# The first projection by quarters, and the constants behind the second and third weight blocks

## The chip, the cores and the metric

One core of a Trainium2 chip runs the whole program in one launch. The metric is the device time of one execution in microseconds (us), lower is better. The kernel before took 724.19 us as the median of three runs (722.73 to 724.41).

## The reference

A two-layer transformer over 256 tokens of width 1024, in float32. Layer 0 is a differential attention with eight heads, followed by a mixture of 32 experts (two chosen per token); layer 1 is a latent attention (MLA) and a second mixture. Only the start of layer 0 is touched here:

```python
q, k, v = jnp.split(x @ w_qkv, 3, axis=-1)          # x: 256 x 1024, w_qkv: 1024 x 3072
...
logits = einsum('bqhcd,bkhcd->bhcqk', q, k)          # two score maps for each of 8 heads
logits = where(chunk_causal, logits - slopes * dist, -inf)
p = softmax(logits)
a = p[:, :, 0] - lam_full * p[:, :, 1]               # lam_full from exp of two dot products
o = rmsnorm(a @ v, subln_g) * (1 - lambda_init)      # then @ w_o, residual, layer norm, experts
```

## The kernel before, in words

All five engines run programs written out by hand; each waits on semaphores. There is no scheduler: the order in the source is the order of execution on each engine, and an instruction that waits holds up all that stand behind it on its engine.

**Split products.** A float32 product is made of three products in a rounded format: operand `a` is written as `a_hi + a_lo`, and `products` (L580) issues hi·hi, hi·lo and lo·hi. ScalarE (ACT) casts to make the upper part, VectorE (DVE) subtracts to make the remainder, TensorE (PE) multiplies.

**The weights of the first attention** come as six blocks of 1024 x 512 (2 MB each) on SyncE's DMA queue (SP, L440 to L454). Block 0 comes in three pieces: rows of quarter 0, of quarter 1, of quarters 2 and 3 (`ld_qkv0`), with semaphores of their own; blocks 1 to 5 have `ld_qkv[c]`. The large constants `cst` (404.5 KB) are queued between block 1 and block 2. GpSimd (POOL) loads nine small tensors (`load_small`, L2209): the triangle and the distance matrix, `diff_lambda`, the router's bias, and the scales of the norms as columns. It begins when the first piece of block 0 has landed. These transfers share the 16 DMA engines with the weights.

**The order at the start.** PE runs 14 dummy products (`keep_clock(START_WAIT)`), transposes `x` (L577) into four PSUM banks, waits for all four remainders of `x` (`x_copied`), runs 8 dummy products (`FIRST_WAIT`), and then goes through four quarters of the inner dimension: for each it waits for the remainder of the weights (`w_lo_ready`) and issues 24 products, so 96 for block 0. ACT casts the four parts of `x` (L1190) and then the four quarters of block 0 (L1208). DVE makes the four remainders of `x` (L1687) and then the four of the weights (L1707).

**Behind it.** PE runs `project_heads(1, 0..2)` (24 products each, block 1), `scores(0)`, `project_heads(1, 3)`, `scores(1)`, `project_values(2, ...)` and so on, with the softmax of head h between the products of later blocks. ACT: `upper(1)`, `move(0)`, `upper(2)`, `move(2)`, `upper(3, (0, 1))`, `exps(0)`, ... DVE: `lower(1)`, `move(1)`, `lower(2)`, `constants()`, `lower(3, (0, 1))`, `logits(0)`, `move(3)`, `lambda_ready()`, ... Here `upper` and `lower` are the cast and the subtraction of a quarter of a block (L1216, L1714), `move(g)` copies a finished group out of PSUM, `logits(h)` takes the maxima of head h (L1736), `exps(h)` the exponentials (L1230), `probabilities(h)` (L1750) the difference of the two maps. PE's `scores(0)` waits for `lam_ready`, the last step of `constants()`. `transposes(h)` (L657) waits for `probabilities(h)`; `values(0)` waits for `move(5)` (L1702).

**After the attention,** the loads of the experts' weights are issued by SP when PE has finished given groups (`qkv_ps`, `wo_ps`, `gu_ps`).

Of the kernel before, what the change touches and what calls it, by code (L numbers as in the profile page):

```python
# [30 lines left out]
ALU = mybir.AluOpType  # L31
# [3 lines left out]
P = 128  # L35
SEQ = 256
TT = SEQ // P
D = 1024
KD = D // P
# [29 lines left out]
RAW_BANKS = ((4, 5, 2, 3), (4, 5, 6, 7))  # L69
ROW_BANK = (6, 3)  # L70
REST_BANK = (4, 6)
START_WAIT, FIRST_WAIT, NORM_WAIT, TOP_WAIT, SORT_WAIT = 14, 8, (11, 0), 6, 8


GU = KD * FF
# [11 lines left out]
CONSTS = _at  # L87
# [62 lines left out]
def build(nc, consts, x, diff_w_qkv, diff_lambda, diff_subln_g, diff_w_o, mla_w_kv_a, mla_kv_norm_g, mla_w_kv_b,  # L150
          mla_w_q_a, mla_q_norm_g, mla_w_q_b, mla_w_o, router_w, router_b, moe_w_gate, moe_w_up, moe_w_down,
          ln_g, ln_b, out):
    with ExitStack() as ctx:
# [10 lines left out]
        def sem(name):  # L164
            return ctx.enter_context(nc.semaphore(name))


        ring, ring_r = zip(*(sb_and_rounded(f"ring{s}", [P, SLOT]) for s in range(SLOTS)))
        xs = sb("x_res", [P, TT, D])
        xT, xT_r = sb_and_rounded("x_T", [P, KD, SEQ])  # L170
# [38 lines left out]
        def qkv_chunk(r, c):  # L209
            a = (c % 3) * 4096  # L210
            return r[2 - c // 3][:, a:a + 4096].rearrange("p (k n) -> p k n", k=KD)
# [110 lines left out]


        ld_x, ld_wo, ld_rw = sem("ld_x"), sem("ld_wo"), sem("ld_router")
        MISC = 8
        ld_ident, ld_cst, ld_misc, ld_lam = sem("ld_ident"), sem("ld_cst"), sem("ld_misc"), sem("ld_lam")

        x_hi_ready, w_hi_ready, w_lo_ready, w_pool_ready = (
            sem(n) for n in ("x_hi_ready", "w_hi_ready", "w_lo_ready", "w_pool_ready"))
# [16 lines left out]
        def x_copied(n):  # L346
            return xt[0]["sb"], KD * {0: 1, 1: 2, 3: 3}[n]
# [94 lines left out]
        def _(sp):  # L442
# [6 lines left out]
            for c in range(1, 6):  # L449
                cols = slice(QKV_COLS[c] * 512, (QKV_COLS[c] + 1) * 512)  # L450
                sp.dma_start(qkv_chunk(ring, c), wq[:, :, cols]).then_inc(ld_qkv[c], 16)
                if c == 1:
                    sp.dma_start(cst[:, P:], consts[:, P:CONSTS]).then_inc(ld_cst, 16)

            def load_wo(w, at_):
# [104 lines left out]
        def _(pe):  # L560
# [8 lines left out]
            def transpose_x(n):  # L569

                for t in range(TT):
                    if n:
                        keep_clock(NORM_WAIT[t], (4, 0)[t])
                        pe.wait_ge(*ln[n - 1]("norm", (1, 3)[t]))
                    for k in range(KD):
                        at_ = (k % 2) * SEQ + t * P
                        last = pe.transpose(psum[:, 4 + k // 2, at_:at_ + P], xs[:, t, k::KD], ident)  # L577
                        if t and k % 2:
                            last.then_inc(xt[n]["ps"], 1)
                if n != 2:  # L580
                    pe.wait_ge(*x_copied(n))

            def products(dst, lhsT, rhs, first, last):

                (a_hi, a_lo), (b_hi, b_lo) = lhsT, rhs
                mm(dst, a_hi, b_hi, first, False)
                mm(dst, a_hi, b_lo, False, False)
                return mm(dst, a_lo, b_hi, False, last)

            def diff_attention():  # L590
# [5 lines left out]

                keep_clock(FIRST_WAIT, 0)
                for q in range(4):
                    pe.wait_ge(w_lo_ready, q + 1)
                    for m in range(4):  # L600
                        for k in (2 * q, 2 * q + 1):
                            cols = slice(m * P, (m + 1) * P)
                            last = products(psum[:, m, 0:SEQ], (w_hi[:, 0, k, cols], qkv_chunk(ring_r, 0)[:, k, cols]),
                                            (xT_r[:, k, :], x_lo[:, k, :]), k == 0, k == KD - 1)
                        if q == 3 and m % 2:
                            last.then_inc(qkv_ps, 1)
                def project_heads(c, m):
                    g = 2 * c + m // 2
                    if m % 2 == 0 and g >= 4:
# [544 lines left out]
        def _(act):  # L1154
# [30 lines left out]
                normalise(1, slice(0, D // 2))  # L1185

            def diff_attention():
                for b in range(4):
                    act.wait_ge(*xt[0]("ps", b + 1))
                    act.copy(xT_r[:, 2 * b:2 * b + 2, :], psum[:, 4 + b, :].rearrange("p (k t) -> p k t", k=2))\  # L1190
                       .then_inc(x_hi_ready, 1)

                def move(g):

# [7 lines left out]
                        c = g // 6  # L1202
                        act.copy(v[:, 0, c * 512:(c + 1) * 512], psum[:, 6, :]).then_inc(qkv_act, 1)

                for q in range(4):
                    act.wait_ge(ld_qkv0[min(q, 2)], 16)
                    rows = slice(2 * q, 2 * q + 2)
                    act.copy(w_hi[:, 0, rows, :], qkv_chunk(ring, 0)[:, rows, :]).then_inc(w_hi_ready, 1)  # L1208
                def upper(c, ms):

                    for m in ms:
# [290 lines left out]
            act.copy(ln_sd[:, 0:1], eps[:, :])  # L1502

            diff_attention()
            act.wait_ge(ld_misc, 16 * MISC)
            moe(0)
            sum_layer_norm(1)
            mla_attention()
# [7 lines left out]
        def _(dve):  # L1516
# [155 lines left out]
                dve.memset(eps[:, :], EPS).then_inc(lam_ready, 1)  # L1672
            def constants():
                dve.wait_ge(ld_cst, 16)
                dve.tensor_copy(ones_b[:, :], ones).then_inc(cast_ready, 1)
                dve.wait_ge(ld_misc, 16 * MISC)
                dve.tensor_copy(tri_b[:, :], tri_f).then_inc(cast_ready, 1)
                dve.tensor_copy(dist_b[:, :], dist_f)

                dve.wait_ge(ld_lam, 16)  # L1680
                chain(dve.tensor_tensor(lam_prod, lam_in[:, 0::2, :], lam_in[:, 1::2, :], ALU.mult))
                dve.tensor_reduce(lam_dot, lam_prod, AX.X, ALU.add).then_inc(lam_ready, 1)

            def diff_attention():
                for b in range(4):
                    dve.wait_ge(x_hi_ready, b + 1)
                    dve.tensor_tensor(x_lo[:, 2 * b:2 * b + 2, :], psum[:, 4 + b, :].rearrange("p (k t) -> p k t", k=2),  # L1687
                                      xT_r[:, 2 * b:2 * b + 2, :], ALU.subtract).then_inc(xt[0]["sb"], 2)

                def move(g):  # L1690

                    dve.wait_ge(qkv_ps, g + 1)
                    src, kind = qkv_heads(g), g // 2 % 3
                    if kind == 0:
                        dve.tensor_scalar(qT[:, heads_of(g), :], src, DH ** -0.5, None, ALU.mult).then_inc(qkv_dve, 1)
                    elif kind == 1:
                        dve.tensor_copy(kT[:, heads_of(g), :], src).then_inc(qkv_dve, 1)
                    else:
                        c = g // 6
                        if c:  # L1700
                            dve.wait_ge(cast_ready, 3)
                        dve.tensor_copy(v[:, 1, c * 512:(c + 1) * 512], psum[:, 7, :]).then_inc(qkv_dve, 1)  # L1702

                for q in range(4):
                    dve.wait_ge(w_hi_ready, q + 1)
                    rows = slice(2 * q, 2 * q + 2)
                    dve.tensor_tensor(qkv_chunk(ring_r, 0)[:, rows, :], qkv_chunk(ring, 0)[:, rows, :],  # L1707
                                      w_hi[:, 0, rows, :], ALU.subtract).then_inc(w_lo_ready, 1)
                def lower(c, ms):

                    for m in ms:
# [5 lines left out]
                def lambda_ready():  # L1717

                    dve.wait_ge(lam_exp, 1)
                    chain(dve.tensor_tensor(nlam[:, :], lam_dot[:, 1:2], lam_dot[:, 0:1], ALU.subtract))  # L1720
                    chain(dve.tensor_scalar(nlam[:, :], nlam[:, :], LAMBDA_INIT, None, ALU.subtract))
                    chain(dve.tensor_scalar(subg[:, :], subg[:, :], 1.0 - LAMBDA_INIT, None, ALU.mult))
# [55 lines left out]

                lower(1, range(4))
                move(1)  # L1780
                lower(2, range(4))
                constants()
                lower(3, (0, 1))
                dve.wait_ge(lam_ready, 2)
                logits(0)
# [349 lines left out]
        def _(pool):  # L2135
# [72 lines left out]

            def load_small():  # L2209

                pool.dma_start(tri_f, consts[:, CONSTS:CONSTS + P]).then_inc(ld_misc, 16)
                pool.dma_start(dist_f, consts[:, CONSTS + P:CONSTS + 4 * P]).then_inc(ld_misc, 16)
                pool.dma_start(lam_in, diff_lambda[0].partition_broadcast(P)).then_inc(ld_lam, 16)
                pool.dma_start(rb[:, :], router_b.partition_broadcast(P)).then_inc(ld_misc, 16)
                with nc.allow_non_contiguous_dma(reason="norm scales as columns, once"):
                    pool.dma_start(subg[:, :], diff_subln_g[0].rearrange("(p a) -> p a", a=1)).then_inc(ld_misc, 16)
                    pool.dma_start(qg[:, :], mla_q_norm_g[0].rearrange("(k p) -> p k", p=P)).then_inc(ld_misc, 16)
                    pool.dma_start(kvg[:, :], mla_kv_norm_g.rearrange("(k p) -> p k", p=P)).then_inc(ld_misc, 16)
                    for col, w in ((gcol, ln_g), (bcol, ln_b)):
                        pool.dma_start(col[:, :, :], w.rearrange("l j (p k) -> p (l j) k", k=KD)[:, 0:3, :])\  # L2220
                          .then_inc(ld_misc, 16)

            pool.wait_ge(ld_qkv0[0], 16)
            load_small()

            def squares(h):
# [11 lines left out]
                pool.dma_start(rw, router_w.rearrange("(p k) n -> p k n", k=KD)).then_inc(ld_rw, 16)  # L2238

            pool.wait_ge(ld_ident, 16)  # L2240
            for h in range(4):
                slopes(h)
            squares(0)
            slopes(4)
# [45 lines left out]
```

## Time and profile before

| | |
|---|---|
| median of three runs | 724.19 us |
| the profiled execution: its own time / span | 722.91 us / 721.1 us |
| granted TensorE clock, mean | 0.987 |
| PE busy | 679.4 us, 94% |
| DVE / ACT / POOL busy | 331.2 / 212.4 / 129.6 us |
| DMA | 237.66 MB, mean 330 GB/s |

The profile is one execution. Times are from the start of its span. In a timeline each row is: start, duration, engine, line, operation, tiles, count, and in brackets how long the engine was idle before and what ended that. Rows of like instructions are merged, so that a row's start plus its duration is the end of the last of them; neighbouring instructions of one engine overlap by some tens of ns.

### The profile page before, as it was taken

Reading aid. Unit: us, or ns where it says so; the run is one execution under the profiler, and the core shown is the slowest. Engines: PE = TensorE matmul, PEld = TensorE weight load, DVE = VectorE, ACT = ScalarE, POOL = GpSimd, SP = SyncE. Lnnn points to the kernel's source line nnn. Section 1 sums busy time; section 2 is a strip of 40 time slices with the busy share of each in tenths; the row PEclk is TensorE's granted clock in tenths of the full one; section 3 lists DMA queues with packets and bytes.
Section 4 is the critical chain, followed back from the end, with each engine's and each line's share of the span. In section 5 each row is a group of like instructions: output and inputs, shape, how many; then the busy total and the mean of one; then the engine's idle time right before and its main releaser. Section 6 shows DMA issues by size and latency. Waiting matters only on the chain.

```text
span 721.1 us, 9996 instructions
## 1 busy us (share of the span) xinstructions
PE 679.4 (94%) x3617; PEld 384.5 (53%) x3617; DVE 331.2 (46%) x679; ACT 212.4 (29%) x416; POOL 129.6 (18%) x143
## 2 busy tenths in 40 slices
PE   7999999889999999999989898988999999999993
PEld 5879878463343343435546776846333334333551
DVE  4658755743434233242274755674343423323226
ACT  4558660421111111111155145342111211112112
POOL 4004010152110010100029560015211101010000
PEclk9999999999999999999999999999999999999997
DMA  8990049959999999999995019385999999999991
GB/s 304 381 357 2 1 187 402 372 204 359 425 421 422 422 420 422 422 422 422 423 413 202 0 44 422 126 349 215 360 424 421 421 421 422 422 422 422 420 404 62
DMA packets 40168, 237.66 MB, mean 330 GB/s; under 512 B 3824, under 2 KB 4000, under 8 KB 15040
## 3 DMA queue, kind: packets, MB, share of 16 engines
q1 hardware_dynamic: 39120, 235.37, 80.1%
q10 hardware_dynamic: 576, 1.05, 0.4%
q0 software_dynamic: 432, 0.70, 0.4%
q8 instruction: 25, 0.41, 0.2%
q14 instruction: 15, 0.12, 0.0%
HBM read 236.06 MB, written 1.05 MB: 329 GB/s over the span
## 4 chain that ended last, share of the span: by engine, by line
PE 88%; DVE 7%; issue 2%; ACT 2%; POOL 1%; POOLq 0%; DVEq 0%; ACTq 0%
PE psum L562 85%; PE psum L1022 2%; POOL scratch L2182 1%; DVE ln_stats L1616 1%; DVE work L1953 1%; DVE work L431 1%; PE psum L872 1%; ACT scratch L1471 0%; PE psum L577 0%; PE psum L657 0%; DVE x_T L1581 0%; POOLq L2166 0%; DVE scratch L1906 0%; DVE ring_rounded L1687 0%; DVE small L1909 0%
## 5 line engine op out<-in xcount | busy, mean ns | idle before, releaser
L562 PE MATMUL psum<-ring,work 128*64 128x512 f32 (+2 forms) x1296 | 231.3, 506 | 3.9 <-DVE work L2047 3.9
L562 PEld LDWEIGHTS psum<-ring,work 128*64 128x64 f32 (+1 forms) x1296 | 94.3, 138 | 137.9 <-issue 116.8
L562 PE MATMUL psum<-ring,scratch 128*64 128x512 f32 x512 | 116.9, 598 | 3.7 <-ACT scratch L1471 3.7
L2089 DVE TENSOR_TENSOR scratch<-psum,scratch 128x256 f32<-128x256 f32 x32 | 13.6, 425 | 183.2 <-ACT scratch L1467 183.2
L2167 POOL COPY work<-work 128x512 f32 x60 | 37.4, 626 | 302.5 <-PE psum L562 295.8
L1460 ACT ACTIVATE x_T_rounded<-psum,small 128x512 fp32r<-128x512 f32 x64 | 43.8, 688 | 110.1 <-DVE scratch_rounded L2070 75.7
L562 PEld LDWEIGHTS psum<-ring,scratch 128*64 128x64 f32 x512 | 33.9, 136 | 68.8 <-issue 63.6
L1467 ACT ACTIVATE scratch<-psum 128x256 f32<-128x256 f32 x32 | 12.3, 384 | 195.1 <-PE psum L562 195.1
L562 PE MATMUL psum<-ring_rounded 128*128 128x256 f32 (+1 forms) x214 | 66.1, 309 | 0.0
L562 PE MATMUL psum<-x_T_rounded,scratch_rounded 128*128 128x512 f32 x144 | 63.1, 438 | 1.9 <-ACT x_T_rounded L1460 1.4
L562 PE MATMUL psum<-ring_rounded,x_T_rounded 128*128 128x512 f32 x192 | 60.7, 397 | 0.0
L562 PE MATMUL psum<-x_T_rounded,ring_rounded 128*128 128x256 f32 x256 | 48.0, 286 | 0.0
L562 PEld LDWEIGHTS psum<-x_T_rounded,scratch_rounded 128*128 128x128 f32 x144 | 29.5, 205 | 31.0 <-issue 28.1
L562 PEld LDWEIGHTS psum<-ring_rounded 128*128 128x128 f32 x214 | 41.5, 194 | 2.0
L562 PEld LDWEIGHTS psum<-x_T_rounded,ring_rounded 128*128 128x128 f32 x256 | 40.4, 192 | 0.8 <-DVE ring_rounded L1714 0.3
L562 PEld LDWEIGHTS psum<-ring_rounded,x_T_rounded 128*128 128x128 f32 x192 | 35.3, 189 | 8.0 <-issue 1.3
L2074 DVE SCALAR_TENSOR_TENSOR work_rounded<-psum,small,x_T_rounded 128x512 fp32r<-128x512 f32 x32 | 24.0, 751 | 28.3 <-ACT x_T_rounded L1460 28.3
L2074 DVE SCALAR_TENSOR_TENSOR scratch_rounded<-psum,small,x_T_rounded 128x512 fp32r<-128x512 f32 x32 | 24.0, 750 | 16.2 <-ACT x_T_rounded L1460 15.9
L2061 DVE SCALAR_TENSOR_TENSOR scratch<-x_T,cst 128x256 f32<-128x256 f32 x32 | 15.7, 491 | 27.2 <-PE psum L562 27.2
L1714 DVE TENSOR_TENSOR ring_rounded<-ring,ring_rounded 128x1024 fp32r<-128x1024 f32 x20 | 23.8, 1241 | 8.1 <-ACT ring_rounded L1216 8.1
L562 PE MATMUL psum<-scratch_rounded 128*128 128x512 f32 x64 | 25.3, 396 | 0.0
L562 PE MATMUL psum<-work_rounded,scratch_rounded 128*128 128x512 f32 x64 | 25.3, 396 | 0.0
(265 smaller groups left out, 850.0 us busy)
## 6 DMA issues: line engine op xcount, KB each, us to landing
ring<-in_moe_w_gate SPq DMA_DIRECT2D x64, 1024.0 KB, 15.6
ring<-in_moe_w_up SPq DMA_DIRECT2D x64, 1024.0 KB, 19.6
ring<-in_moe_w_down SPq DMA_DIRECT2D x64, 1024.0 KB, 20.6
ring<-in_diff_w_qkv SPq DMA_DIRECT2D x5, 2048.0 KB, 19.5
ring<-in_diff_w_o SPq DMA_DIRECT2D x1, 4096.0 KB, 15.7
ring<-in_mla_w_o SPq DMA_DIRECT2D x1, 4096.0 KB, 35.3
ring<-in_mla_w_q_b SPq DMA_DIRECT2D x1, 2304.0 KB, 28.9
ring<-in_mla_w_kv_b SPq DMA_DIRECT2D x1, 2048.0 KB, 27.8
```

The source lines that it names most:

```text
L431: link(eng.tensor_tensor(dst[:, :, lo], src[:, :, lo], c, ALU.mult))
L562: return pe.matmul(dst, lhsT, rhs, start=start, stop=stop, skip_group_check=True)
L872: last = pe.transpose(psum[:, 2 + h % 2, b * P:(b + 1) * P], mlg[h % 3][:, b * P:(b + 1) * P], ident)
L1022: last = pe.transpose(psum[:, 7, k * P:(k + 1) * P], h_sb[:, k::FF // P], ident)
L1460: act.activation(y_hi[:, c * 512:(c + 1) * 512], psum[:, 4 + c, :], ACT.Copy, scale=gate_col)\
L1467: act.activation(act_s, psum[:, 6, 0:FF], ACT.Silu).then_inc(m["s_ready"], 1)
L1616: chain(dve.bn_stats(ln_stats[:, t, c, :], psum[:, 2 * t + c, :]))
L1714: dve.tensor_tensor(qkv_chunk(ring_r, c)[:, :, cols], qkv_chunk(ring, c)[:, :, cols], w_hi[:, c % 2, :, cols], ALU.subtract).then_inc(w_lo ...
L2061: dve.scalar_tensor_tensor(out=comb, in0=key_row[:, 0, :], scalar=at_, in1=gate_row[:, 0, :], op0=ALU.is_equal, op1=ALU.mult).then_inc(par ...
L2074: dve.scalar_tensor_tensor(out=y_lo[c], in0=psum[:, 4 + c, :], scalar=gate_col, in1=y_hi[:, c * 512:(c + 1) * 512], op0=ALU.mult, op1=ALU. ...
L2089: dve.tensor_tensor(h_sb, psum[:, 6, FF:2 * FF], act_s, ALU.mult).then_inc(m["h_ready"], 1)
L2167: last = pool.tensor_copy(xg[:, buf, :, j * WIN:(j + 1) * WIN], xsT[:, :, bass.ds(a, WIN)])
```

## The change

Block 0 is worked on by quarters on ACT and DVE (cast of `x`, cast of weights; remainder of `x`, remainder of weights), and PE issues in each quarter first the eight hi·hi products, then the eight with the remainder of `x`, then the eight with the remainder of the weights, each with its own wait. PE no longer waits for all of `x_lo`, and runs 3 dummy products instead of 8. `cst` is queued behind block 2. POOL's transfers wait for block 1 instead of the first piece of block 0; the six for scales and the router's bias are issued later still, behind the first two `slopes`. On DVE `constants()` stands ahead of `lower(2)`, and waits for `cst` and the three small tensors.

```diff
-START_WAIT, FIRST_WAIT, NORM_WAIT, TOP_WAIT, SORT_WAIT = 14, 8, (11, 0), 6, 8
+START_WAIT, FIRST_WAIT, NORM_WAIT, TOP_WAIT, SORT_WAIT = 14, 3, (11, 0), 6, 8
@@ sync
                 sp.dma_start(qkv_chunk(ring, c), wq[:, :, cols]).then_inc(ld_qkv[c], 16)
-                if c == 1:
+                if c == 2:
                     sp.dma_start(cst[:, P:], consts[:, P:CONSTS]).then_inc(ld_cst, 16)
@@ tensor
-                if n != 2:
-                    pe.wait_ge(*x_copied(n))
...
                 for q in range(4):
+                    def first_products(w, src, first, last):
+                        for m in range(4):
+                            for k in (2 * q, 2 * q + 1):
+                                done = mm(psum[:, m, 0:SEQ], w[:, k, m * P:(m + 1) * P], src[:, k, :],
+                                          first and k == 0, last and k == KD - 1)
+                            if last and q == 3 and m % 2:
+                                done.then_inc(qkv_ps, 1)
+                    pe.wait_ge(w_hi_ready, q + 1)
+                    first_products(w_hi[:, 0], xT_r, True, False)
+                    pe.wait_ge(*xt[0]("sb", 2 * (q + 1)))
+                    first_products(w_hi[:, 0], x_lo, False, False)
                     pe.wait_ge(w_lo_ready, q + 1)
-                    for m in range(4):
-                        for k in (2 * q, 2 * q + 1):
-                            cols = slice(m * P, (m + 1) * P)
-                            last = products(psum[:, m, 0:SEQ], (w_hi[:, 0, k, cols], qkv_chunk(ring_r, 0)[:, k, cols]),
-                                            (xT_r[:, k, :], x_lo[:, k, :]), k == 0, k == KD - 1)
-                        if q == 3 and m % 2:
-                            last.then_inc(qkv_ps, 1)
+                    first_products(qkv_chunk(ring_r, 0), xT_r, False, True)
@@ scalar
+                for q in range(4):
+                    rows = slice(2 * q, 2 * q + 2)
+                    act.wait_ge(*xt[0]("ps", q + 1))
+                    act.copy(xT_r[:, rows, :], psum[:, 4 + q, :].rearrange("p (k t) -> p k t", k=2)).then_inc(x_hi_ready, 1)
+                    act.wait_ge(ld_qkv0[min(q, 2)], 16)
+                    act.copy(w_hi[:, 0, rows, :], qkv_chunk(ring, 0)[:, rows, :]).then_inc(w_hi_ready, 1)
@@ vector: remainders of x and of the weights in one loop over q, in the same way; constants() ahead of lower(2)
             def constants():
                 dve.wait_ge(ld_cst, 16)
+                dve.wait_ge(ld_small, 16 * 3)
...
                 def lambda_ready():
                     dve.wait_ge(lam_exp, 1)
+                    dve.wait_ge(ld_scales, 16 * SCALES)
@@ gpsimd
-            pool.wait_ge(ld_qkv0[0], 16)
+            pool.wait_ge(ld_qkv[1], 16)
             load_small()                      # now three transfers: triangle, distances, lambda
             pool.wait_ge(ld_ident, 16)
-            for h in range(4):
+            for h in range(2):
+                slopes(h)
+            load_scales()                     # the other six
+            for h in range(2, 4):
                 slopes(h)
```

## Rows read from the trace of the kernel before

**Rows 1.** Chain that ended last, in order of time: start, us, what (count).

```profile
11.35 22.06 PE psum L562 x176
33.41 1.22 issue
47.34 0.33 PE psum L657 x3
```

**Rows 2.** The same chain by engine, from the page.

```profile
PE 88%; DVE 7%; issue 2%; ACT 2%; POOL 1%; POOLq 0%; DVEq 0%; ACTq 0%
```

**Rows 3.** Timeline of TensorE: dummy products, first products, then values(0) and values(2).

```profile
11.35 1.90 PE L562 MATMUL psum<-zeros_b 128*128 128x512 bf16 x8 [2.60 <-DVE ring_rounded L1687]
...
13.21 0.28 PE L562 MATMUL psum<-ring_rounded 128*128 128x256 f32 x1
...
13.57 0.28 PE L562 MATMUL psum<-ring_rounded 128*128 128x256 f32 x1
...
57.55 0.83 PE L562 MATMUL psum<-work,scratch 128*128 128x128 f32 x6
...
65.30 0.83 PE L562 MATMUL psum<-work,scratch 128*128 128x128 f32 x6
```

**Rows 4.** Timeline of ScalarE, 0 to 65 us.

```profile
8.12 2.06 ACT L1190 CAST x_T_rounded<-psum 128x512 fp32r<-128x512 f32 x4 [5.83 <-PE psum L577]
10.03 4.14 ACT L1208 CAST ring_rounded<-ring 128x1024 fp32r<-128x1024 f32 x4
12.17 2.00 ACT L1208 CAST ring_rounded<-ring 128x1024 fp32r<-128x1024 f32 x2
21.38 3.90 ACT L1216 CAST ring_rounded<-ring 128x1024 fp32r<-128x1024 f32 x4 [7.21 <-DMA ring<-in_diff_w_qkv]
...
27.76 3.90 ACT L1216 CAST ring_rounded<-ring 128x1024 fp32r<-128x1024 f32 x4 [1.99 <-DMA ring<-in_diff_w_qkv]
...
33.18 1.99 ACT L1216 CAST ring_rounded<-ring 128x1024 fp32r<-128x1024 f32 x2 [1.05 <-DMA ring<-in_diff_w_qkv]
...
63.49 0.37 ACT L1241 COPY work<-psum 128x256 f32<-128x256 f32 x1
```

**Rows 5.** Timeline of VectorE, 0 to 60 us.

```profile
8.81 2.48 DVE L1687 TENSOR_TENSOR ring_rounded<-psum,x_T_rounded 128x512 fp32r<-128x512 f32 x4 [7.61 <-ACT x_T_rounded L1190]
...
28.84 4.63 DVE L1714 TENSOR_TENSOR ring_rounded<-ring,ring_rounded 128x1024 fp32r<-128x1024 f32 x4 [1.14 <-ACT ring_rounded L1216]
...
34.45 2.35 DVE L1714 TENSOR_TENSOR ring_rounded<-ring,ring_rounded 128x1024 fp32r<-128x1024 f32 x2
36.71 1.02 DVE L1736 TENSOR_REDUCE small<-psum 128x2 f32<-128x256 f32 x2
...
44.07 0.75 DVE L1750 SCALAR_TENSOR_TENSOR scratch<-scratch,small 128x128 f32<-128x128 f32 x2 [2.47 <-ACT scratch L1237]
...
51.69 1.02 DVE L1736 TENSOR_REDUCE small<-psum 128x2 f32<-128x256 f32 x2 [0.45 <-PE psum L562]
...
55.85 0.69 DVE L1702 COPY work<-psum 128x512 f32<-128x512 f32 x1
```

**Rows 6.** Timeline of GpSimd: first and third of the nine small transfers issued.

```profile
8.38 0.73 POOL L2211 DMA_DIRECT2D work<-in_shape_constants  x1 [7.88 <-DMA ring<-in_diff_w_qkv]
...
9.64 0.56 POOL L2213 DMA_DIRECT2D scratch<-in_diff_lambda  x1
```

**Rows 7.** DMA issues of two small transfers: KB, us from issue to landing.

```profile
scratch<-in_diff_lambda POOLq DMA_DIRECT2D x1, 128.0 KB, 7.3
ln_b_cols<-in_ln_b POOLq DMA_DIRECT2D x1, 12.0 KB, 8.1
```

**Rows 8.** Stretches: busy us of each engine (instructions), granted clock, DMA share, GB/s.

```profile
16.00:18.00 2.00, 2.00 (x19) 2.00 (x18) 0.02 (x1) 0.00 (x0) 0.41 (x1) 1.00 0.85 274
...
24.00:26.00 2.00, 2.00 (x19) 2.00 (x18) 2.00 (x3) 1.77 (x3) 0.00 (x0) 1.00 1.06 389
```

**Rows 9.** Waits of SyncE's queue up to 160 us: in total, times, longest.

```profile
SPq L466 <- PE psum L562: 90.9, 3, 59.0
```

More of the change, by code:

```diff
@@ L324, in build @@
         ld_x, ld_wo, ld_rw = sem("ld_x"), sem("ld_wo"), sem("ld_router")
-        MISC = 8
-        ld_ident, ld_cst, ld_misc, ld_lam = sem("ld_ident"), sem("ld_cst"), sem("ld_misc"), sem("ld_lam")
+        SCALES = 6
+        ld_ident, ld_cst, ld_scales, ld_small = sem("ld_ident"), sem("ld_cst"), sem("ld_scales"), sem("ld_small")
         x_hi_ready, w_hi_ready, w_lo_ready, w_pool_ready = (
@@ L1187, in diff_attention @@
             def diff_attention():
[L1188 to L1191, printed above, removed]
+                for q in range(4):
[4 more added lines that the diff above has]
+                    act.copy(w_hi[:, 0, rows, :], qkv_chunk(ring, 0)[:, rows, :]).then_inc(w_hi_ready, 1)
                 def move(g):
@@ L1203, in move @@
                         act.copy(v[:, 0, c * 512:(c + 1) * 512], psum[:, 6, :]).then_inc(qkv_act, 1)
[L1205 to L1208, printed above, removed]
                 def upper(c, ms):
@@ L1504, in _ @@
             diff_attention()
-            act.wait_ge(ld_misc, 16 * MISC)
+            act.wait_ge(ld_scales, 16 * SCALES)
             moe(0)
@@ L1674, in constants @@
                 dve.wait_ge(ld_cst, 16)
+                dve.wait_ge(ld_small, 16 * 3)
                 dve.tensor_copy(ones_b[:, :], ones).then_inc(cast_ready, 1)
-                dve.wait_ge(ld_misc, 16 * MISC)
                 dve.tensor_copy(tri_b[:, :], tri_f).then_inc(cast_ready, 1)
                 dve.tensor_copy(dist_b[:, :], dist_f)
-                dve.wait_ge(ld_lam, 16)
                 chain(dve.tensor_tensor(lam_prod, lam_in[:, 0::2, :], lam_in[:, 1::2, :], ALU.mult))
@@ L1684, in diff_attention @@
             def diff_attention():
[L1685 to L1688, printed above, removed]
+                for q in range(4):
+                    rows = slice(2 * q, 2 * q + 2)
+                    dve.wait_ge(x_hi_ready, q + 1)
+                    dve.tensor_tensor(x_lo[:, rows, :], psum[:, 4 + q, :].rearrange("p (k t) -> p k t", k=2),
+                                      xT_r[:, rows, :], ALU.subtract).then_inc(xt[0]["sb"], 2)
+                    dve.wait_ge(w_hi_ready, q + 1)
+                    dve.tensor_tensor(qkv_chunk(ring_r, 0)[:, rows, :], qkv_chunk(ring, 0)[:, rows, :],
+                                      w_hi[:, 0, rows, :], ALU.subtract).then_inc(w_lo_ready, 1)
                 def move(g):
@@ L1702, in move @@
                         dve.tensor_copy(v[:, 1, c * 512:(c + 1) * 512], psum[:, 7, :]).then_inc(qkv_dve, 1)
[L1704 to L1708, printed above, removed]
                 def lower(c, ms):
@@ L1780, in diff_attention @@
                 move(1)
+                constants()
                 lower(2, range(4))
-                constants()
                 lower(3, (0, 1))
@@ L2209, in load_small, with load_scales @@
             def load_small():
[L2211 to L2214, printed above, removed]
+                pool.dma_start(tri_f, consts[:, CONSTS:CONSTS + P]).then_inc(ld_small, 16)
+                pool.dma_start(dist_f, consts[:, CONSTS + P:CONSTS + 4 * P]).then_inc(ld_small, 16)
+                pool.dma_start(lam_in, diff_lambda[0].partition_broadcast(P)).then_inc(ld_small, 16)
+            def load_scales():
+                pool.dma_start(rb[:, :], router_b.partition_broadcast(P)).then_inc(ld_scales, 16)
                 with nc.allow_non_contiguous_dma(reason="norm scales as columns, once"):
-                    pool.dma_start(subg[:, :], diff_subln_g[0].rearrange("(p a) -> p a", a=1)).then_inc(ld_misc, 16)
-                    pool.dma_start(qg[:, :], mla_q_norm_g[0].rearrange("(k p) -> p k", p=P)).then_inc(ld_misc, 16)
-                    pool.dma_start(kvg[:, :], mla_kv_norm_g.rearrange("(k p) -> p k", p=P)).then_inc(ld_misc, 16)
+                    pool.dma_start(subg[:, :], diff_subln_g[0].rearrange("(p a) -> p a", a=1)).then_inc(ld_scales, 16)
+                    pool.dma_start(qg[:, :], mla_q_norm_g[0].rearrange("(k p) -> p k", p=P)).then_inc(ld_scales, 16)
+                    pool.dma_start(kvg[:, :], mla_kv_norm_g.rearrange("(k p) -> p k", p=P)).then_inc(ld_scales, 16)
                     for col, w in ((gcol, ln_g), (bcol, ln_b)):
                         pool.dma_start(col[:, :, :], w.rearrange("l j (p k) -> p (l j) k", k=KD)[:, 0:3, :])\
-                          .then_inc(ld_misc, 16)
-            pool.wait_ge(ld_qkv0[0], 16)
+                          .then_inc(ld_scales, 16)
+            pool.wait_ge(ld_qkv[1], 16)
             load_small()
```

## The prediction

> **What bounds the kernel now.** I read the chain of waits first, then the timelines of the four engines over the first 65 us, and last the DMA views. The chain is TensorE for 88% [rows 2]; what isn't TensorE near the change is small: between the transposes of x and the first product TensorE idles 2.60 us and then runs eight dummy products, and at 33.41 it stops for 1.22 us before the scores of head 0 [rows 1, 3]. From 34.63 to about 98 us it has no gap. So at the start the end is set by TensorE, and time comes only from an earlier start or from that stop. Behind the attention the loads of the experts' weights are issued when TensorE is through with a group: SyncE's queue waited 90.9 us for it in three waits [rows 9]. A shift at 98 us therefore moves transfers and products together, and I carry it to the end unchanged.
>
> **Part 1, the start.** The regular beat of block 0 is three products in 13.57 - 13.21 = 0.36 us, 0.12 each; by it the first issues at 13.1 [rows 3]. After the change the first eight need the cast of x (8.12 plus 2.06 / 4 = 0.52) and one weight cast (4.14 / 4 = 1.03) [rows 4]: 9.7 us. The three dummies (1.90 / 8 = 0.24 each) end before that. So TensorE starts 13.1 - 9.75 = 3.3 us sooner. It stays fed: a quarter costs TensorE 24 x 0.12 = 2.9 us, ScalarE 0.52 + 1.03 = 1.55, VectorE 2.48 / 4 + 4.63 / 4 = 1.78 [rows 4, 5]. The third piece of block 0 lets its cast begin at 12.17 [rows 4]; TensorE wants it at 9.75 + 5.8 = 15.5. The number of products stays 96, each with its own weight load. Their beat in the new order isn't in the trace: at 0.12 it costs nothing, and at 0.15 it would cost 2.9 us, of which the slack found in part 4 hides 2.5. So I take 0, and neither end moves the sum by more than 0.4. Block 0 ends at 21.3.
>
> **Part 2, block 1.** It lands at 21.38 now, 9.2 us behind the last piece of block 0; blocks 2 and 3 are 5.4 us apart (27.76, 33.18) [rows 4]. The 3.8 us between are the nine small transfers: throughput falls to 274 GB/s at 16 to 18 us, against 389 later [rows 8]. With them gone block 1 lands at 12.17 + 5.4 = 17.6 at best and 21.4 at worst. TensorE needs its first quarter cast and subtracted (0.97 + 1.16) at 21.3, so a landing by 19.1 is in time. I take 17.7. The 72 products ahead of scores(0) then end at 30.1 instead of 33.4.
>
> **Part 3, the constants.** VectorE's constants() take 34.45 - (28.84 + 4.54) = 1.1 us and now stand ahead of lower(2) [rows 5]. They wait for lambda, issued 1.26 us after the start of POOL's transfers and landing 7.3 later [rows 6, 7]: 17.7 + 8.6 = 26.3. They also wait for cst, queued behind block 2. All bytes that must have landed by then are those that have landed at 27.76 now, so cst comes at 27.8 at the latest, about 26.5 as I see it. Block 2 itself comes at 25 to 26.7. Behind the waiting VectorE stands lower(2), 4 x 1.15 us, and behind that lower(3), logits(0) and all of the softmax. Constants from 26.5 mean lower(2) from 27.6 to 32.2: before the casts of block 3. lam_ready comes at 27.6, so the stop of 1.22 us goes, and TensorE stands at scores(0) at 30.1: 4.5 us ahead of before. The six scale transfers are issued at about 21.7 to 25.9 and land by 34 (8.1 us for the last [rows 7]); lambda_ready() wants them at 39.4, so this added wait costs 0.
>
> By the Trainium skill, page DMA: Bandwidth & Descriptors, section on the anatomy of one DMA on the GpSimd path, such a transfer takes about 2.0 us plus its bytes over the bandwidth, an estimate of 2.3 us for lambda. The row has 7.3 beside full queues; the row decides, and by the page the rival of late constants below would fall away.
>
> **Part 4, what is late next.** The lead of 4.5 us can't be kept. logits(0) stands on VectorE behind lower(3, (0, 1)), which needs block 3. All small transfers have passed by then before and after, so block 3 lands at about 33.2 again; its first cast is done at 34.2. Before, VectorE began lower(3) at 34.45, held by the constants; now at 34.27. So logits(0) goes from 36.71 to 36.5, a gain of 0.2 [rows 5]. From there the softmax is a chain of VectorE and ScalarE that TensorE doesn't hold up. probabilities(0), done at 44.8 before, come at 44.6; TensorE used them at 47.3 [rows 1, 5], 2.5 us of slack, and can't be more than 2.7 ahead there. The next place is tighter: logits(3) at 51.69 had waited 0.45 us for TensorE [rows 5], which now is early, so it gains 0.2 + 0.45 and about 0.1 of overlap: 0.75. move(5) at 55.85 goes to 55.1 and ends at 55.8; values(0), at 57.55 before, waits for it: it comes at 55.8, **1.75 us** sooner [rows 3, 5]. The stops at scores(2), transposes(0) and values(0), 2.7 us together, are where the rest of the 4.5 goes.
>
> Behind values(0) I looked for tighter places. values(2) at 65.30 needs ScalarE's copy of 63.49 plus 0.37 [rows 3, 4]: the copy gains 0.75 and is done at 63.1, TensorE comes at 63.55. The slack of 0.4 holds. The rest of the attention's waits have over 0.5 us.
>
> **The sum.** 722.91 - 1.75 = 721.2 for the profiled execution; that execution lies 1.3 below the median of the three runs, so against the median 724.19 - 1.75 = **722.4 us**, 0.24% less. About 0.3% (2.2 us) is what a measurement of this kernel can tell from no change; the forecast lies just inside it.
>
> **The rivals.**
>
> *Block 3 lands sooner.* The dip in throughput came with the scale columns. They are now issued 11 to 13 us later, the last lands near 33, so part of the loss may fall behind block 3. For: block 3 has 5.4 us per block and could be as early as 30.5 with no loss from the columns (17.6 + 2 x 5.4 + 1.1 for cst + 1.0 for small bytes). Against: the dip began some 6 us behind the first issue, by which it ends at 31. Each us earlier is one us more, up to the 4.5: at 1 us, 2.75 gained, 721.4.
>
> *The whole lead survives* (the softmax isn't as tight as I think, or block 3 comes at 30.5): 4.5 gained, 719.7.
>
> *Late constants, slower.* VectorE waits at constants() with lower(2) and the softmax behind it. Free until 28.5; at 30.2 all the gain is used up, since move(5) has then lost the 1.0 us of slack that values(0) had (57.55 against 56.54) plus the 0.7 that the chain has to spare. It decides if block 1 lands as late as before: 21.4, plus 1.3, plus 7.3 is 30.0; with the 8.1 us of the last column instead of 7.3, 30.8, and that is 0.6 us slower than before, 724.8; every further us one more. For: 7.3 us is measured in like traffic. Against: block 1 was late because of what is moved away.
>
> *The clock.* Three dummies instead of eight, and three new stops of TensorE. If the granted clock fell to its lower level (1.2 GHz), a product would take 0.12 us more; 37 of them use up the 4.5 us, all 96 of block 0 make it about 7 us slower than before at scores(0), 731. Against: the idle time of 2.60 us before the dummies [rows 3] left the granted clock at 1.00, and the new gaps are shorter (0.7, 1.3 and 0.7 us). The Trainium skill, page TensorE: Matmul & The Clock Gate, section Why this matters for your kernels, warns that gaps between bursts of matmuls put the engine back to its slow level; the trace shows that the one gap here didn't.
>
> **How the numbers follow.** Forecast (gain 1.0 to 2.2): 0.44. Block 3 sooner: 0.26. The whole lead: 0.08. Late constants: 0.16, of which 0.12 still within 0.3% of before. The clock or a stall that I don't see: 0.06, slower. Faster by over 0.3%: 0.26 + 0.08 = 0.34, and I add 0.02 from the upper edge of the forecast: 0.36. Slower: 0.04 + 0.06 = 0.10. Same: 0.54. The range: the whole lead less nothing is 719.7, late constants to 0.6 slower 724.8; the runs' own spread of 1.7 lies within that.
>
> **What would show it.** The first real product at 9.75; no wait between quarters; block 1's casts at 17.7 (over 19.1 part 2 is wrong); VectorE's constants at 26 to 27.8; no stop before scores(0) at 30; logits(0) at 36.5, and TensorE's waits at transposes(0) on VectorE's L1750 and at values(0) on its copy. Block 3's first cast tells the rivals apart: 33.2 is the forecast. A granted clock under 1.00 in the first 60 us, or constants behind 28.5, would make the prediction wrong.

## The result and the profile after

The changed kernel took 719.38 us (median of six runs, 718.24 to 720.07), the kernel before in the same series 723.15 us (six runs): a ratio of 0.9941, 95% interval 0.9925 to 0.9958, so 3.8 us less by the medians and 4.3 by the ratio, where 1.75 was forecast. The measured time lies just under the range. The forecast counted from 724.19 us, the median of the first three runs before; with three more it is 723.15, so 1.0 us of the distance to 722.4 isn't owed to the change. The profiled execution took 719.77 us, its span is 717.5.

Timeline of TensorE after (columns as before: start, duration, what, idle time before it and what ended it); it answers to [rows 1, 3].

```profile
8.62 0.81 PE L562 MATMUL psum<-zeros_b 128*128 128x512 bf16 x3
9.74 1.22 PE L562 MATMUL psum<-x_T_rounded,ring_rounded 128*128 128x256 f32 x8 [0.31 <-ACT ring_rounded L1199]
...
30.00 0.50 PE L562 MATMUL psum<-dist_b,slope 128*128 128x384 bf16 x2
...
43.79 0.55 PE L663 MATMUL psum<-cst,scratch 128*128 128x128 f32 x3 [0.94 <-DVE scratch L1753]
...
55.01 0.91 PE L562 MATMUL psum<-work,scratch 128*128 128x128 f32 x6 [0.61 <-issue]
```

The start is as planned: the first product at 9.74, no wait inside block 0, the scores of head 0 at 30.00 without a stop (34.63 before). Then the lead of 4.6 us shrinks: 0.94 us are lost at transposes(0), 0.61 at values(0), the rest in gaps too short to be listed. values(0) comes at 55.01, 2.54 us sooner than before.

Timeline of ScalarE after: the first cast of the third piece of block 0 and the casts of blocks 1, 2 and 3, each released by its transfer; it answers to [rows 4].

```profile
12.21 1.05 ACT L1199 CAST ring_rounded<-ring 128x1024 fp32r<-128x1024 f32 x1 [0.59 <-DMA ring<-in_diff_w_qkv]
...
17.63 3.89 ACT L1220 CAST ring_rounded<-ring 128x1024 fp32r<-128x1024 f32 x4 [2.94 <-DMA ring<-in_diff_w_qkv]
...
24.89 3.90 ACT L1220 CAST ring_rounded<-ring 128x1024 fp32r<-128x1024 f32 x4 [2.87 <-DMA ring<-in_diff_w_qkv]
...
32.34 2.00 ACT L1220 CAST ring_rounded<-ring 128x1024 fp32r<-128x1024 f32 x2 [3.08 <-DMA ring<-in_diff_w_qkv]
```

Timeline of VectorE after: constants, lower(2), lower(3), logits(0), logits(3), move(5); it answers to [rows 5].

```profile
25.94 0.23 DVE L1680 CAST ones_b<-cst 128x128 bf16<-128x128 f32 x1 [1.74 <-DMA cst<-in_shape_constants]
...
27.01 4.62 DVE L1716 TENSOR_TENSOR ring_rounded<-ring,ring_rounded 128x1024 fp32r<-128x1024 f32 x4
33.42 2.36 DVE L1716 TENSOR_TENSOR ring_rounded<-ring,ring_rounded 128x1024 fp32r<-128x1024 f32 x2 [1.79 <-ACT ring_rounded L1220]
35.70 1.01 DVE L1739 TENSOR_REDUCE small<-psum 128x2 f32<-128x256 f32 x2
...
50.08 1.01 DVE L1739 TENSOR_REDUCE small<-psum 128x2 f32<-128x256 f32 x2
...
54.23 0.68 DVE L1709 COPY work<-psum 128x512 f32<-128x512 f32 x1
```

lower(3) is now released by the cast of block 3, and logits(0) follows at once. The chain that ended last says the same. It no longer runs over TensorE in this stretch:

```profile
12.08 20.24 DMA ring<-in_diff_w_qkv
32.34 1.06 ACT ring_rounded L1220
33.42 0.98 DVE ring_rounded L1716
34.59 1.11 issue
35.70 1.02 DVE small L1739 x2
```

By engine, after, as [rows 2]: the path has a share of DMA that it didn't have.

```profile
PE 83%; DVE 8%; DMA 3%; ACT 2%; issue 2%; SPq 2%; DVEq 0%; ACTq 0%
```

Two questions stand: why the attention gained 2.5 us and not 1.75, and where the other 1.2 to 1.7 us of the measured gain come from (the expectations below call them 1.4). In the two profiled executions the spans differ by 3.6 us: 2.5 up to the end of the attention (98.4 before, 95.9 after) and 1.1 behind it, and the granted clock is 1.00 up to 100 us in both.

### The profile page after: what moved, and what is told of

The parts are those of the page before. It is cut to its first block, busy times and chain, and to the rows that moved or that the text cites. A ratio compares the mean times of both kernels' runs of the same rounds, so it can differ in the third digit from the quotient of the medians.

```text
span 717.5 us, 9984 instructions
## 1 busy us (share of the span) xinstructions
PE 678.2 (95%) x3608; PEld 383.3 (53%) x3612; DVE 331.1 (46%) x679; ACT 212.1 (30%) x416; POOL 129.3 (18%) x143
## 4 chain that ended last, share of the span: by engine, by line
PE 83%; DVE 8%; DMA 3%; ACT 2%; issue 2%; SPq 2%; DVEq 0%; ACTq 0%
PE psum L562 80%; DMA ring<-in_diff_w_qkv 3%; PE psum L1028 2%; DVE work L1956 1%; DVE ln_stats L1620 1%; DVE work L431 1%; SPq L451 1%; PE psum L878 1%; SPq L453 1%; ACT scratch L1234 0%; ACT scratch L1475 0%; PE psum L663 0%; DVE x_T L1585 0%; DVE small L1739 0%; DVE scratch L1909 0%
## 5 line engine op out<-in xcount | busy, mean ns | idle before, releaser
L562 PE MATMUL psum<-ring,work 128*64 128x512 f32 (+2 forms) x1296 | 234.0, 512 | 3.9 <-DVE work L2050 3.9
L562 PE MATMUL psum<-ring_rounded 128*128 128x256 f32 (+1 forms) x214 | 61.7, 310 | 0.0
L562 PE MATMUL psum<-x_T_rounded,ring_rounded 128*128 128x256 f32 x256 | 44.7, 285 | 0.3 <-ACT ring_rounded L1199 0.3
L562 PEld LDWEIGHTS psum<-ring_rounded 128*128 128x128 f32 x214 | 39.6, 194 | 2.0
L562 PEld LDWEIGHTS psum<-x_T_rounded,ring_rounded 128*128 128x128 f32 x256 | 38.4, 192 | 1.5 <-ACT ring_rounded L1199 0.8
## 6 DMA issues: line engine op xcount, KB each, us to landing
ring<-in_moe_w_up SPq DMA_DIRECT2D x64, 1024.0 KB, 19.5
ring<-in_moe_w_down SPq DMA_DIRECT2D x64, 1024.0 KB, 20.4
```

What stands on the lines that cost most here:

```text
L562: return pe.matmul(dst, lhsT, rhs, start=start, stop=stop, skip_group_check=True)
```

## The experiments

Eleven runs follow, eight of new kernels and three that repeat the changed kernel or the one before. Ratios are against the kernel before on the same chip, with 95% intervals.

**The quarters alone.** The kernel before with these edits of block 0, and no transfer moved:

```diff
-START_WAIT, FIRST_WAIT, ... = 14, 8, ...
+START_WAIT, FIRST_WAIT, ... = 14, 3, ...
+ the loops over q of TensorE, ScalarE and VectorE as in the change; no wait for all of x_lo
```

> The kernel before with the quarters and 3 dummies alone; every transfer and constants() as before. Theory (block 3 and VectorE's order set the softmax, and the landing of block 1 and lam_ready hold TensorE before it): block 1 still lands at 21.4, TensorE waits for it with products that end at 21.3, and stops again before scores(0), which stays at 34.6; values(0) stays at 57.5; the time is that of before within 0.3 us. Rival (an earlier start of TensorE is worth what it is by itself): scores(0) at 31.3 and values(0) at 54.2, 3.3 us faster.

0.9992 (0.9978 to 1.0005): nothing gained. The first product is at 9.74, block 1's cast at 20.54, and TensorE's timeline shows where the 3 us stay:

```profile
33.93 0.48 PE L562 MATMUL psum<-dist_b,slope 128*128 128x384 bf16 x2 [2.15 <-issue]
...
58.39 0.83 PE L562 MATMUL psum<-work,scratch 128*128 128x128 f32 x6
```

The stop before scores(0) grew from 1.22 to 2.15 us; what ends it is lam_ready (VectorE's last constant ends at 33.84). The stops are those of the theory, but all of it stands some 0.7 us sooner than said: block 1 landed 0.8 sooner in this execution, and block 3's cast began at 32.47 for 33.18, with no transfer moved. And values(0) is at 58.39, although scores(0) is 0.7 sooner than before: the granted clock fell in this execution, which no expectation had. From scores(0) to values(0) it took 24.46 us, 22.92 before [rows 3], so the fall cost 1.5 us. Stretches of it (busy us by engine, then clock, DMA share, GB/s):

```profile
28.00:36.00 8.00, 5.85 (x43) 4.71 (x42) 7.83 (x11) 5.43 (x7) 0.11 (x1) 0.91 1.05 387
36.00:44.00 8.00, 8.00 (x47) 6.58 (x47) 3.43 (x11) 5.34 (x19) 1.01 (x2) 0.87 1.03 370
```

**The transfers alone.** The changed kernel with block 0 in the old order:

```diff
+ 8 dummies, wait for all of x_lo, casts and remainders of x ahead of those of the weights, hi·hi, hi·lo, lo·hi by turns
```

> The changed kernel with the order of block 0 (casts, remainders, products, 8 dummies, the wait for all remainders of x) as before; the transfers and constants() as changed. Theory: the first product at 13.1, no stop before scores(0), which comes at 33.3; block 3's cast at 32.3; values(0) at 56.2 to 56.3, TensorE the bound, so 1.3 us faster than before. With the quarters' 0 alone the two parts then sum to 1.3, less than the 2.5 of both. Rival (the two parts add up): with 0 for the quarters this one would have to give 2.5, values(0) at 55.0.

0.9967 (0.9952 to 0.9981), 2.4 us. The profile was as expected: first product at 13.30, scores(0) at 33.64 with no stop, block 3's cast at 32.33, values(0) at 56.58: 1.0 sooner than before, or 1.4 if the late start of this execution is taken off (its dummies begin at 11.75, 11.35 before [rows 3]). So in the attention the transfers alone give 1.0 to 1.4 and both parts together 2.5. The quarters alone give 0 by the measured time and by the theory's count; their one profile, with the fallen clock, can't confirm it. The measured 2.4 is more than that; here too something is gained that the profile of the attention doesn't show.

**The change once more.**

> The changed kernel once more, to size the effect and to see what repeats. Theory: up to the end of the attention at 96 us the profile repeats within 0.2 us (values(0) at 55.0), and the rest of the span scatters by about 1 us with the places at which the granted clock falls; the ratio comes nearer to 2.5 us less than before (0.9965) than to the 3.8 of the first runs. Rival: the change is worth 3.8 us (0.9948) by something behind the attention that repeats: the span between the attention's end and the end of the program is again 1.1 us shorter than before.

0.9946 (0.993 to 0.9961), 3.9 us (3.1 by the medians, where the first series had 4.3 and 3.8). values(0) at 55.30, with the whole start 0.30 late (first product at 10.04); the stops are 0.95 and 0.64. The attention repeats. The ratio stays near that of the first series, against the theory. The rival fares no better: from the end of the attention to the end of the span it is 622.3 us, against 621.6 in the first profile after and 622.7 before.

**The scale transfers late.**

```diff
-            for h in range(2):
+            for h in range(4):
                 slopes(h)
+            pool.wait_ge(ld_qkv[4], 16)
             load_scales()                     # five of the six; subg goes with load_small
```

> The changed kernel with five of the six scale transfers behind block 4 instead of behind block 1 (the scale of the sub-norm goes with the three small ones). Theory (the softmax of head 0 follows block 3, and the scale columns cost block 3 about 0.9 us): block 3's first cast at 31.4 instead of 32.3, logits(0) at 34.8, values(0) at 54.1 to 54.3, 0.8 us faster than the changed kernel. Rival 1 (the columns cost the weights nothing): 32.3 and 55.0 again. Rival 2 (block 3 isn't what values(0) waits for): block 3 sooner and values(0) at 55.0.

```profile
17.35 3.89 ACT L1220 CAST ring_rounded<-ring 128x1024 fp32r<-128x1024 f32 x4 [2.94 <-DMA ring<-in_diff_w_qkv]
...
31.43 2.00 ACT L1220 CAST ring_rounded<-ring 128x1024 fp32r<-128x1024 f32 x2 [2.00 <-DMA ring<-in_diff_w_qkv]
```

```profile
42.89 0.55 PE L663 MATMUL psum<-cst,scratch 128*128 128x128 f32 x3 [0.47 <-DVE scratch L1752]
...
54.12 0.91 PE L562 MATMUL psum<-work,scratch 128*128 128x128 f32 x6 [0.62 <-issue]
```

Block 3's cast began at 31.43, transposes(0) at 42.89, values(0) at 54.12, each 0.9 sooner than in the changed kernel. 0.28 of that is an earlier start of all transfers in this execution (block 1 at 17.35 for 17.63), so by this pair the columns cost block 3 some 0.6. values(0) followed block 3. The ratio of 0.9931 (0.9915 to 0.9948) points the same way (0.9946 in the same series), but the intervals overlap: the time alone doesn't show it.

**TensorE later.** `FIRST_WAIT` 17 instead of 3 in the changed kernel.

> The changed kernel with 17 dummy products ahead of block 0 instead of 3, so that its products start about 2.6 us later (12.3 instead of 9.7). Theory (behind block 3 the softmax sets TensorE's time, and TensorE has 0.94 + 0.61 us of stops plus up to 0.2 more to give): the stops vanish and values(0) comes 0.9 us later than in the changed kernel, at 55.9. Rival (TensorE's start sets it): 2.6 later, at 57.6.

```profile
8.67 3.83 PE L562 MATMUL psum<-zeros_b 128*128 128x512 bf16 x17
12.15 1.30 PE L562 MATMUL psum<-x_T_rounded,ring_rounded 128*128 128x256 f32 x8
...
55.43 0.83 PE L562 MATMUL psum<-work,scratch 128*128 128x128 f32 x6
```

2.4 us later at the start, 0.4 later at values(0), with no stop on the way; ratio 0.9935 (0.9915 to 0.9955), no slower than the changed kernel. So of the 3.3 us that the quarters bring forward, 2.0 were of no use. The theory holds; the slack was 2.0, not 1.7.

**The softmax ahead of block 3.** The same instructions in another order:

```diff
@@ scalar
-                upper(3, (0, 1))
                 exps(0)
...
-                upper(3, (2, 3))
+                upper(3, (0, 1))
                 exps(1)
                 scale_second(0)
+                upper(3, (2,))
                 exps(2)
...
                 move(4)
+                upper(3, (3,))
@@ vector
-                lower(3, (0, 1))
                 dve.wait_ge(lam_ready, 2)
                 logits(0)
...
+                lower(3, (0,))
                 logits(1)
+                lower(3, (1,))
```

> The changed kernel with the softmax of heads 0 and 1 ahead of the casts and remainders of block 3 on ScalarE and VectorE, which move into the idle time behind; the instructions are the same. Theory (it was the order that tied the softmax to block 3): logits(0) at 31.5 instead of 35.7 though block 3 still comes at 32.3; TensorE's stops at transposes(0) and values(0) go; values(0) at 52.9 to 53.2, 2 us sooner, and the kernel 2 us faster than the changed one. Rival (the bound is the softmax's own work or TensorE's wait for a later block): values(0) stays within 0.5 of 55.0.

**0.9893 (0.9872 to 0.9914)**, 716.29 us: about twice the gain of the change. VectorE and TensorE:

```profile
31.69 1.01 DVE L1740 TENSOR_REDUCE small<-psum 128x2 f32<-128x256 f32 x2
```

```profile
29.64 0.50 PE L562 MATMUL psum<-dist_b,slope 128*128 128x384 bf16 x2
...
52.58 0.83 PE L562 MATMUL psum<-work,scratch 128*128 128x128 f32 x6
```

logits(0) stands at 31.69, before block 3 has landed (at 32.4, issued at 12.0 and landed 20.4 later); scores(0) to values(0) is 22.94 us, the 22.92 of the kernel before without a stop (57.55 - 34.63) [rows 1, 3]. All of the lead survives. The two stops are gone.

**Both.**

> The softmax first and the scale transfers late, together. Theory: with the order undone the landing of block 3 no longer counts, so values(0) stands where the softmax first alone puts it (within 0.2 us) and the 0.9 of the late scales isn't added. Rival (the two gains are of different causes and add): values(0) 0.9 sooner still.

0.9897 (0.9877 to 0.9917); values(0) at 52.83, and 43.20 us behind its first product as in the one before (52.58 - 9.40 = 43.18). Block 3 landed 1.1 us sooner than in that run (31.4 for 32.4), and values(0) didn't follow. The late scales add nothing once nothing waits for block 3. That is the theory.

**The later work where it stood before.** The changed kernel with

```diff
                 pe.wait_ge(ot_sb, 4)
+                keep_clock(12)
```

> The changed kernel with 12 dummy products (2.6 us) near the end of the attention, so that all that follows stands about where it stands in the kernel before. It asks where the 1.4 us come from that the changed kernel gains beyond its 2.5 at the end of the attention. Theory (they come from where in time the work behind the attention falls, which moves the stretches with a lower granted clock): the time is that of the kernel before, ratio 0.999 to 1.001, mean clock 0.987 as before. Rival (they belong to the changed kernel wherever it stands): 2.6 slower than the changed kernel, 722.6 to 722.9, ratio 0.998 to 0.9985, mean clock 0.9885.

The first mean and variance of the layer norm were at 123.02 (122.76 before), so the shift worked. The ratio is 0.9963 (0.9945 to 0.9981), the mean clock 0.9892. The theory falls: with the later work in its old place the kernel is still 2.7 us faster than before. The rival's 0.998 to 0.9985 lies at the edge of the interval; against the changed kernel's 0.9941 and 0.9946 the shift cost 1.2 to 1.6 us, less than the 2.6 put in. In this profile two stretches behind the attention have a clock under 1.00 ahead of the last one, three in the changed kernel's; a place in time may matter, but the other way round, and this stays open. From that first mean and variance to the end of the span it is 595.4 us, against 598.3 in the first profile before: in this pair of profiles the whole gain lies behind the attention.

**The idle time filled.** The kernel before with

```diff
+                if n == 0:
+                    keep_clock(11, 0)
                 if n != 2:
                     pe.wait_ge(*x_copied(n))
...
                     if h == 0:
+                        keep_clock(5)
                         pe.wait_ge(lam_ready, 2)
```

> The kernel before with dummy products where TensorE idles: 11 while it waits for the remainders of x (2.60 us) and 5 at its stop before scores(0) (1.22 us). Nothing else starts sooner or later: values(0) at 57.5. It asks where the 1.4 us come from that the changed kernel gains beyond its attention. Theory (in many executions of the kernel before, though not in the profiled one, the granted clock falls after these idle times, as it did at 28 to 44 us in the run of the quarters alone; the changed kernel doesn't idle there): mean clock 0.988 to 0.989 instead of 0.9865, 1.0 to 1.4 us faster than before, ratio 0.998 to 0.9987. Rival (the difference arises behind the attention): mean clock 0.9865 and ratio 0.9995 to 1.0005.

0.9981 (0.9965 to 0.9998), 1.4 us faster, mean clock 0.9885 over 12 runs (0.9873 in the 17 of before in this series, 0.9866 and 0.9861 in the two others). values(0) at 57.70: no work came sooner. The two idle times shrank to 0.22 and 0.64 us. Sixteen more dummy products made the kernel faster. That bears the theory out in time and clock, but the interval reaches into the rival's range (0.9995), and the profile speaks for the rival too: the clock was at 1.00 up to 100 us, as in the first profile before, the first mean and variance of the layer norm came at 122.91 (122.76 before), and from there to the end it took 596.9 us instead of 598.3. The first difference in the clock lies here (columns as above), the kernel before above, this one below:

```profile
120.00:160.00 40.00, 35.06 (x179) 24.14 (x179) 24.21 (x73) 12.61 (x19) 10.21 (x15) 0.96 0.73 292
```

```profile
120.00:160.00 40.00, 34.07 (x185) 23.94 (x186) 24.39 (x75) 13.07 (x20) 10.69 (x15) 1.00 0.75 299
```

**The kernel before, twice more,** unchanged.

> The kernel before once more, for its profile. Theory as in the run with filled idle times: if the clock fell early in this execution, a stretch under 1.00 stands between 25 and 60 us and the attention ends later than 98.4. Rival: clock 1.00 up to 100 us again, and what differs from the first profile lies behind 120 us.

> The same once more, with the same expectations; of the two at least one should show the early stretch if the theory holds for half of the executions.

The first took 723.80 us, with values(0) at 57.48 and a clock of 1.00 up to 100 us. The second took 725.53: TensorE's row and the stretch behind it, and below it the same stretch of the first.

```profile
34.96 0.48 PE L562 MATMUL psum<-dist_b,slope 128*128 128x384 bf16 x2 [1.98 <-issue]
...
59.39 0.83 PE L562 MATMUL psum<-work,scratch 128*128 128x128 f32 x6
```

```profile
36.00:44.00 8.00, 8.00 (x47) 6.73 (x44) 4.46 (x11) 4.34 (x14) 1.62 (x2) 0.79 0.96 335
```

```profile
36.00:44.00 8.00, 8.00 (x56) 6.20 (x55) 4.04 (x12) 6.09 (x21) 1.62 (x2) 1.00 1.05 388
```

After a stop of 1.98 us the clock went to its lower level (1.2 GHz) for part of that stretch (0.79 on average, 47 products recorded for 56), and values(0) came 1.9 us later than in the other. 0.4 of that was there at scores(0) already (34.96 for 34.54, block 1 having landed 0.4 later); from scores(0) to values(0) it took 24.43 us instead of 22.94, so the fall cost 1.5 us. Some executions of the kernel before lose that, and the profile on which the forecast rests was one that didn't. It is a part of the missing 1.4 us. It isn't shown to be all of it: one profile in three is 0.5 us on average, and behind the attention the profiles differ as well:

| run | clock up to 100 us | clock, 120 to 160 us | from the first mean and variance to the end of the span |
|---|---|---|---|
| before, three profiles | 1.00, 1.00, 0.98 | 0.96 in all | 598.3, 598.8, 599.1 |
| idle time filled | 1.00 | 1.00 | 596.9 |
| changed, two profiles | 1.00, 1.00 | 0.96, 1.00 | 597.3, 597.9 |

## Why the prediction was wrong

**Part 1, right.** First product at 9.74 for 9.75; no wait between quarters; the beat is 0.12 in the new order too.

**Part 2, right.** Block 1 at 17.63 for 17.7.

**Part 3, right.** cst at 25.9 for 26.5, constants 1.07 us, lam_ready at 27.1, scores(0) at 30.00 for 30.1. The late constants of the rival didn't come: lambda landed 5.9 us behind its issue, not 7.3.

**Part 4, the mechanism right, one term mis-sized.** The step "so block 3 lands at about 33.2 again" failed: it came at 32.34. The gain of logits(0) was 1.01 us, not 0.2. It is the 0.2 in the term 0.2 + 0.45 + 0.1. What stood on top came out as worked: logits(3) gained 1.61, that is 1.01 plus 0.60 for the 0.45 of waiting and the overlap (0.55 was said), and values(0) 2.54. The rival "block 3 lands sooner" with "each us earlier is one us more" is what happened. The small transfers cost the weights less than before: from the third piece of block 0 to block 3 it was 21.0 us before [rows 4] and is 20.1 now. One pair alone would prove little, since the quarters alone had 20.4 with every transfer in its old place. Over all profiles it was 20.4 to 21.8 with the small transfers in the old place (five executions), 20.1 to 20.7 in the new one (six), and 19.5 and 19.6 with the columns late. Why the same bytes cost some 0.8 less in the new place isn't shown. That the softmax and not TensorE sets values(0) is shown by three runs: TensorE 2.4 later moved it by 0.4, block 3 0.9 sooner by 0.9, and the order undone by 2.4 (0.3 of it an earlier start).

**The sum, wrong by a term that isn't in it.** With 2.54 us instead of 1.75 the sum would have been 721.65, still inside the range. What is left is 1.2 to 1.7 us of gain, and the 1.0 us by which the median of the first three runs before lay above that of all six. The prediction took one profiled execution as the kernel before, in which "the idle time of 2.60 us before the dummies [rows 3] left the granted clock at 1.00", and priced the clock only as a risk of the change. That step failed: the clock was a cost of the kernel before too. Filled idle times took 1.4 us off it (0.1 to 2.5 by the interval). The stop before scores(0) is the likelier of the two idle times. Of the four profiled executions that have it, the clock fell in two, and there the fall began 0.7 and 1.3 us behind the end of stops of 2.15 and 1.98 us (estimates from stretches of 1 us); after stops of 1.22 and 0.92 us it didn't. In the nine without it, or with it filled, the clock was 1.00 up to 100 us. The quarters alone, with the longer stop and without the 2.60 us, had a mean clock of 0.9863 over 12 runs; the transfers alone, with the 2.60 us and without the stop, 0.9893.

How much of the 1.2 to 1.7 us this is stays open. The early fall costs 1.5 us where it comes, and it came in one of three profiles of the kernel before. In the first pair of profiles, and in that of the filled idle times, the part behind the attention is 1.1 to 1.4 us shorter with no early fall on either side; the clock there falls at places that change from one execution to the next, and no run shows what sets them.

Here the page TensorE: Matmul & The Clock Gate of the Trainium skill, section Why this matters for your kernels, warns of gaps between bursts of matmuls, and I set it aside on one gap in one execution. The gaps it warns of are longer than the stops of 2.15 and 1.98 us behind which the clock fell here, and the measurement decides. In these runs the same program showed both outcomes.

## What to carry to other kernels

When an engine gets a lead, look for the order on the other engines that ties their next step to a transfer: moving the softmax ahead of the casts of a block not yet landed gave about as much again as the whole change. Two parts that are worth about 0 and 1.0 to 1.4 us by themselves can be worth 2.5 together, since each removes a wait that hides the other. Look at the clock in several profiles of the kernel before, not one, before a gap of TensorE is called free.

## What the runs showed of the hardware

Sixteen dummy products in idle time made the kernel 1.4 us faster (0.1 to 2.5) with no work moved. Between two executions of the same program the granted clock over 36 to 44 us was 1.00 and 0.79, and the stretch from scores(0) to values(0) took 1.5 us more (24.43 for 22.94). With nine small transfers issued ahead of it, block 1 landed 9.2 us behind the last piece of block 0; with them issued later, 5.4.
